# Hybrid NSA, SGU, S5 and expert layers: remaining parts on GpSimd, gates in column groups, four banks for the last rows, output sent by tile

## What is computed

```
for l in range(2):
    h = rms_norm(x, norm_mix_g[l])
    q, k_c, v_c, k_s, v_s, k_w, v_w, nsa_g, sgu_in, s5_in, branch_g = split(h @ w_in[l])
    nsa_gates = sigmoid(nsa_g)                       # 24 columns: 8 heads x 3 branches
    y_a = nsa_attention(q, ..., nsa_gates, positions) @ w_attn_o[l]   # compressed, selected, window
    y_b = spatial_gating(sgu_in, ...) @ w_sgu_o[l]
    y_c = s5_layer(s5_in, ...) @ w_s5_o[l]
    g_a, g_b, g_c = split(sigmoid(branch_g))
    x = x + (g_a * y_a + g_b * y_b + g_c * y_c) @ w_mix_o[l]
    h = rms_norm(x, norm_ffn_g[l])
    x = x + hierarchical_moe(h, ...)                 # 4 groups x 8 experts, top 2 of one group
return rms_norm(x, norm_final_g)
```

## Time and profile before

| | |
|---|---|
| median of 3 runs | 1936.79 us (1935.34 to 1937.72) |
| the profiled execution, its own time | 1934.61 us |
| its span in the trace | 1932.8 us |
| busy share PE / DVE / ACT / POOL | 97% / 51% / 25% / 7% |
| granted TensorE clock, mean | 0.986 of full speed |
| DMA moved | 482.13 MB, 427 GB/s in the slices of the expert phases |

### The profile page before, as it was taken

One profiled execution on the slowest core, in us unless ns is written; L12 is line 12 of the kernel. 1 busy time (PEld: TensorE's weight loads), 2 busy tenths in 40 slices (PEclk: granted clock), 3 DMA queues, 4 the chain that ended last, 5 costly groups with the idle time before them and its releaser, 6 DMA issues. The chain is left out here.

```text
span 1932.8 us, 26668 instructions
## 1 busy us (share of the span) xinstructions
PE 1865.5 (97%) x10360; PEld 1170.3 (61%) x10361; DVE 993.6 (51%) x1929; ACT 479.5 (25%) x854; POOL 144.5 (7%) x237
## 2 busy tenths in 40 slices
PE   6999999999999999999899999999999999999995
PEld 4768777778445455454457777777774445455442
DVE  7764655676344343343467555557673344343344
ACT  4403444423111111111234134444321111111112
POOL 3600000050000000000063000000400000000000
PEclk9999999999999999999989999999999999999998
DMA  4222111253999999999712221114359999999993
GB/s 168 66 81 78 66 66 66 89 159 145 378 427 427 424 427 425 427 428 420 310 50 85 76 83 66 66 45 123 125 218 403 427 427 426 425 425 424 426 428 154
DMA packets 59952, 482.13 MB, mean 249 GB/s; under 512 B 9808, under 2 KB 22608, under 8 KB 30672
## 3 DMA queue, kind: packets, MB, share of 16 engines
q1 hardware_dynamic: 59856, 480.80, 61.3%
HBM read 476.59 MB, written 4.19 MB: 249 GB/s over the span
## 5 line engine op out<-in xcount | busy, mean ns | idle before, releaser
L1877 DVE TENSOR_TENSOR x_tokens<-x_tokens,ps 128x512 f32<-128x512 f32 x240 | 161.7, 687 | 236.7 <-PE ps L1041 235.5
L1107 PE MATMUL ps<-arena,branch 128*64 128x512 f32 x512 | 226.6, 595 | 0.0
L1107 PE MATMUL ps<-slabs,branch 128*64 128x512 f32 x512 | 226.6, 595 | 0.0
L1057 PE MATMUL ps<-arena 128*64 128x512 f32 x512 | 225.1, 592 | 0.5 <-DVE arena L1867 0.5
L1057 PE MATMUL ps<-slabs,arena 128*64 128x512 f32 x512 | 225.0, 592 | 0.5 <-issue 0.5
L1058 PE MATMUL ps<-arena 128*64 128x512 f32 x512 | 225.1, 592 | 0.0
L1058 PE MATMUL ps<-slabs,arena 128*64 128x512 f32 x512 | 225.0, 592 | 0.0
L779 PE MATMUL ps<-h_hi,w_parts 128*128 128x512 f32 x768 | 210.8, 408 | 1.5 <-DVE w_parts L1490 1.5
L1057 PEld LDWEIGHTS ps<-slabs,arena 128*64 128x64 f32 x512 | 70.1, 137 | 146.5 <-issue 146.4
L779 PEld LDWEIGHTS ps<-h_hi,w_parts 128*128 128x128 f32 x768 | 135.1, 189 | 38.8 <-issue 9.2
L1057 PEld LDWEIGHTS ps<-arena 128*64 128x64 f32 x512 | 70.0, 137 | 145.9 <-issue 145.9
(11 more groups left out here) (353 smaller groups left out, 3129.2 us busy)
## 6 DMA issues: line engine op xcount, KB each, us to landing
arena<-in_expert_w_gate SPq DMA_DIRECT2D x32, 2048.0 KB, 12.2
slabs<-in_expert_w_gate SPq DMA_DIRECT2D x32, 2048.0 KB, 15.1
slabs<-in_expert_w_up SPq DMA_DIRECT2D x32, 2048.0 KB, 19.6
arena<-in_expert_w_up SPq DMA_DIRECT2D x32, 2048.0 KB, 16.7
arena<-in_expert_w_down SPq DMA_DIRECT2D x32, 2048.0 KB, 9.5
slabs<-in_expert_w_down SPq DMA_DIRECT2D x32, 2048.0 KB, 14.0
slabs<-in_gate_w SPq DMA_DIRECT2D x24, 1024.0 KB, 4.8
slabs<-in_dense SPq DMA_DIRECT2D x22, 1024.0 KB, 5.8
```

What stands on the lines that cost most here:

```text
L1057: nc.tensor.matmul(ps[0:64, BANK_GU[b], :], xk, low[:, k, :], start=(k == 0), stop=(k == ND - 1), tile_position=(0, 0))
L1107: done = nc.tensor.matmul(ps[64 * b:64 * b + 64, BANK_Y[half], :], hidT[:, k, CAP * b:CAP * (b + 1)], w_down[b][:, k, half * 512:(half + 1 ...
L1877: v.tensor_tensor(xs, xs, ps[:, BANK_BACK[n % 2], :], ALU.add).then_inc(s["back_added"], 1)
```

## The change

Six parts, in both layers unless said:

1. **Prologue.** DVE's angle operations stand between the scalings of tiles (`scale_token(t)`), ACT takes the root of tile t-1 after the square of tile t, and sin is computed before the last angle operations for cos. POOL builds a 128x24 matrix `stack` of four 24-column pieces of the identity, one for each group of 32 rows.
2. **Gates.** `nsa_job` keeps 32 columns of weights as the stationary operand in one of four column groups (`tile_position=(0, r)`), and moves 128 tokens of `hT`; contraction step k goes to group k % 4. ACT copies the 128x512 result to SBUF (`nsa_parts`), and `nsa_sums()`, placed after the two S5 jobs, adds the four groups with four matmuls against `stack`. Tanh stands later on ACT, after `s5_evac(1)`.
3. **Rotation** of index u - 2 in place of u - 1, so each one job later.
4. **Remaining parts.** `low_part` goes from DVE to POOL, in half tiles: a multiplication (L2110: x, read with a stride, by 1/rms) and a subtraction (L2111) of 128x512 each, 16 operations for a layer. `gather_tile` waits for its half tile.
5. **Last quad.** Returned rows use four PSUM banks in place of two; `add_back(0)` stands behind `hid_of(1)`; in the final pair only rows 0 to 3 come before the hidden transposes, then the first half of the down product, rows 4 to 7, and the second half.
6. **Output** (last layer). SP sends each tile in the layer's own block as soon as it is scaled; the last block only waits.

```
 def square_tokens(act, g, arrived):
...
                 nc.scalar.activation(x_unit[:, t, :], x[:, t, :], ACT.Square, accum_out=sumsq[:, t:t + 1]).then_inc(g["sq"], 1)
-                act.wait_ge(g["var"], t + 1)
-                nc.scalar.activation(rstd[:, t:t + 1], sumsq[:, t:t + 1], ACT.Sqrt).then_inc(g["sd"], 1)
+                if t >= 1:
+                    root(t - 1)
+            root(NT - 1)
...
-                reduce_angle(nc, link, ang, kk, rr, r2)
-                scale_tokens(dve, turn_g, False)
+                turns_of(nc, link, ang, kk)
+                link(nc.vector.scalar_tensor_tensor(rr, kk, -PI_1, ang, ALU.mult, ALU.add))
+                scale_token(dve, turn_g, 0, False)
+                link(nc.vector.scalar_tensor_tensor(rr, kk, -PI_2, rr, ALU.mult, ALU.add))
+                scale_token(dve, turn_g, 1, False)
+                link(nc.vector.scalar_tensor_tensor(rr, kk, -PI_3, rr, ALU.mult, ALU.add))
+                link(nc.vector.tensor_scalar(rr, rr, PI_SAFE, -PI_SAFE, ALU.min, ALU.max))
+                scale_token(dve, turn_g, 2, False)
+                scale_token(dve, turn_g, 3, False)
+                quarter_from(nc, link, rr, r2)
...
                     if last_layer:
                         sp.dma_start(gfin, io["gfin"].to_broadcast([P, D])).then_inc(s["gfin_in"], 16)
                         sp.wait_ge(s["gfin_in"], 16)
+                        for t in range(NT):
+                            sp.wait_ge(s["next_xn"], t + 1)
+                            sp.dma_start(io["out"][0, t * P:(t + 1) * P, :], x_unit[:, t, :]).then_inc(fin, 16)
...
                         for k in range(ND):
-                            last = nc.tensor.matmul(ps[:, BANK_S[0], t * 24:(t + 1) * 24], hT[:, k, t * P:(t + 1) * P], wnsa[:, k, :],
-                                                    start=(k == 0), stop=(k == ND - 1))
+                            r = 32 * (k % 4)
+                            last = nc.tensor.matmul(ps[r:r + 32, BANK_S[0], t * P:(t + 1) * P], wnsa[k], hT[:, k, t * P:(t + 1) * P],
+                                                    start=(k < 4), stop=(k >= 4), tile_position=(0, r))
+                        last.then_inc(s["nsa_done"], 1)
+
+                    def nsa_sums():
+
+                        pe.wait_ge(s["nsa_parted"], 1)
+                        for t in range(NT):
+                            last = nc.tensor.matmul(ps[:, BANK_S[1], t * 24:(t + 1) * 24], nsa_parts[:, t * P:(t + 1) * P], stack, start=True, stop=True)
                         last.then_inc(s["nsa_done"], 1)
...
-                        if 1 <= u <= 6:
-                            rotate(u - 1)
+                        if 2 <= u <= 7:
+                            rotate(u - 2)
...
-                                pe.wait_ge(s["x_lo_ready"], t + 1 + (half if t == NT - 1 else 0))
+                                pe.wait_ge(s["x_lo_ready"], 2 * t + half + 1)
...
+                        banks = BANK_BACK_LAST if last_quad else BANK_BACK
+                        final = last_quad and at == 3
+                        for n in range(4 if final else 8):
                             if not first:
                                 if n >= 2 or not second:
-                                    back_free(i, n)
-                                row_back(n)
+                                    back_free(i, n, 4 if final or last_quad and n >= 2 else 2)
+                                row_back(n, banks)
...
+                        down_half(i, 0)
+                        if final:
+                            for n in range(4, 8):
+                                back_free(i, n, 4)
+                                row_back(n, banks)
+                        down_half(i, 1)
...
-                    def low_part(t, lo, hi):
-
-                        dve.wait_ge(s["x_hi_ready"], t + 1)
-                        to, of = (a[:, t, :].rearrange("q (k p) -> q k p", k=ND)[:, lo:hi] for a in (x_lo, x_hi))
-                        xs = x[:, t, :].rearrange("q (p k) -> q k p", k=ND)[:, lo:hi]
-                        v.scalar_tensor_tensor(to, xs, rstd[:, t:t + 1], of, ALU.mult, ALU.subtract).then_inc(s["x_lo_ready"], 1)
...
+                    def low_part(t, half):
+
+                        ks = slice(4 * half, 4 * half + 4)
+                        xs = x[:, t, :].rearrange("q (p k) -> q k p", k=ND)[:, ks]
+                        unit, hi, lo = (a[:, t, :].rearrange("q (k p) -> q k p", k=ND)[:, ks] for a in (xn, x_hi, x_lo))
+                        link(g.tensor_tensor(unit, xs, rstd[:, t:t + 1].unsqueeze(2).to_broadcast([P, 4, P]), ALU.mult))
+                        g.tensor_tensor(lo, unit, hi, ALU.subtract).then_inc(s["x_lo_ready"], 1)
+
+                    for t in range(NT):
+                        pool.wait_ge(s["x_hi_ready"], t + 1)
+                        for half in range(2):
+                            low_part(t, half)
...
-                for t in range(NT):
-                    sp.dma_start(io["out"][0, t * P:(t + 1) * P, :], x_unit[:, t, :]).then_inc(fin, 16)
                 sp.wait_ge(fin, 16 * NT)
```

More of the change, by code:

```diff
@@ L2176, in _ @@
                     def _(dve):
-                        scale_tokens(dve, turn_g, last_layer)
+                        for t in range(NT):
+                            scale_token(dve, turn_g, t, last_layer)
                     @block.tensor
```

112 lines of the change are left out of this document (70 added, 42 removed).

## The result

| | before | after |
|---|---|---|
| median of 4 runs | 1936.35 us (1935.34 to 1937.72) | 1921.73 us (1920.38 to 1923.66) |
| ratio, 95% interval | | 0.9928 [0.9914, 0.9942] |
| profiled execution, its own time | 1934.61 us | 1923.66 us |
| span | 1932.8 us | 1921.9 us |

The change makes the kernel 14.6 us (0.7%) faster. The forecast was 1912.7 us with 1897 to 1920: the direction was right, and the time lies 9 us over the forecast and 1.7 us over the range.

The account below looks back on a forecast made before the run. Edits pay in PE's own work, its waits or the two ends; 1934.61 - 11.2 - 12.2 - 0.7 - 2.4 - 4.8 + 7.2 = 1910.5 us, 1912.7 by the median, range 1897 to 1920.

Parts of the forecast that it names:

- Gates: Gate jobs, both layers: shorter matmuls and the clock staying up behind them, 11.2 us gained, 6.6 if the clock falls.
- Rotation: First rotation, both layers: PE's wait for DVE goes and the clock returns, 12.2 us gained; 7.9 without the clock.
- Prologue: Start of the kernel: scaled tiles come sooner and PE's transposes end earlier, 0.7 us gained (0.3 to 1).
- Last quad: Last expert pair of each layer: PE's waits for a free bank go, twice 1.2 us gained.
- Output: End of the kernel: tiles leave earlier and the last transfer lands in 3.8 us, 4.8 us gained (3.6 to 5.7).
- Remaining parts on POOL: Routing, both layers: POOL's reads delay DVE's routes and PE waits, 3.6 us a layer, 7.2 us lost in all.
- Turn-taking: Forecast case, 54%: in routing, DVE's small two-input operations wait for whole POOL operations; 1912.7 us, own range 1908 to 1919.
- the rival in which it does not come back elsewhere: Rival, 12%: low clock stays at gates and rotation, and falls behind new waits; 1923 us, range 1917 to 1926.
- small operations are not held: Rival, 30%: POOL does not hold DVE's small routing operations, 4.7 us gain for 7.2 loss; 1900.8 us, 1898 to 1903.
- The slower one: Rival, 3%: POOL's strided operations so slow that the gather waits at its last tile; about 1946 us at 4 us each.
- the lower end of its own range, 1908: Forecast case's fastest time, said to come from the unstrided POOL price and the output's bounds.
- the 1.8 us price: Routing: the first POOL operation of each pair, strided, taking 1.8 us, for a loss of 6.4 us a layer.

Follow-up runs that it names:

- gates_one_sum: The kernel before with the gate part alone and one of its four summing matmuls for each layer; 1921.91 us, ratio 0.9932.
- only_pool: The kernel before with the remaining parts moved to POOL and nothing else; 1948.16 us, ratio 1.0076.
- pool_writes: The changed kernel with POOL's two operations for each half tile replaced by five memsets that read nothing; 1906.12 us, ratio 0.9851.
- only_gates: The kernel before with the gate part alone, including the small POOL block that builds `stack`; 1929.69 us, ratio 0.9976.
- after_pair: The changed kernel with the gate jobs of tiles 0 and 1 joined, eight matmuls fewer for each layer; 1917.39 us, ratio 0.9909.
- between_pad16: The kernel with POOL's work placed where DVE does not route, plus 16 already met PE waits before `rank(3)`; 1903.43 us, ratio 0.9838.
- between_pad32: The kernel with POOL's work placed where DVE does not route, plus 32 already met PE waits before `rank(3)`; 1907.36 us, ratio 0.9852.

## Why the prediction was right or wrong

- **Gates: right in mechanism and size, but for what they do to the code.** 2.4 us for the jobs where 2.76 was forecast, and the clock stayed up behind them. `gates_one_sum`, with a short branch and 1.3 us of matmuls too few, is 13.1 us faster than before (10 to 16); less 1.3, 11.8 against 11.2 forecast. That the sizes meet is luck in part: the 4.6 us for the clock were read from one execution in which it fell behind the old gates in both layers, while over the six profiled kernels with the old gates it did so in six places of twelve. With the new gates it did so in none of twenty-two.
- **Rotation: right.** 12.2 us forecast and measured alone, the waits gone and the clock up behind them.
- **Prologue: too small a term, it seems**, 0.7 us (0.3 to 1) against 3 us (1 to 5) alone. Why it is more than the trace's 1.3 us at the in-projection is open; a low clock came in half of the executions there and not in the others.
- **Last quad: not to be told** from nothing alone (forecast 2.4, interval -1.5 to 5.6).
- **Output: too small a term**, 4.8 against 7.2 us (4 to 10) alone, 6.1 in its trace, since a transfer issued by itself landed in 2.6 us and not 3.8. In the changed kernel PE's branch ends the program instead and leaves 3.7.
- **Remaining parts on POOL: the step that failed most.** Turn-taking was the right case: the small operations are held. But the forecast's term, "3.6 us a layer, 7.2 us in all", is 14.7 us alone (10.6 to 19) and 9.3 (medians) to 16 (traces) in the change. It had two waits. PE's wait at `route_logits(1)` was 2.55 for 2.1 us; the held TENSOR_SCALAR, 0.92 us longer than free, was not counted. The wait for `rank(3)` grew by 1.26 us, as forecast within 0.3. These two make 3.8 of the 7.9 us that PE lost in layer 1's routing. The other 4 us, which the term did not have at all, go with the clock: it fell behind the first wait (6.58 us busy at 0.56, 2.9 us lost) and was low for longer before the experts. The forecast had put a low clock after these waits only in the rival in which it does not come back elsewhere. In the four executions in which POOL reads while DVE routes it fell behind both waits in both layers, sixteen places of sixteen. Behind the old wait of about 1.7 us for `rank(3)`, in the eight kernels with the parts on DVE, it fell in eight places of sixteen.
- **The branch: a step that was missing.** The forecast's sum went over engines' work and waits in the program's stages and took the layer's end as it stood. With the gate part PE's branch takes 3.3 to 4.1 us and not 0.35; 3.5 us at the boundary and 2.4 at the end (5.5 against 3.1 us from the last scaling to the end of the span).

Put together from the parts alone: -3.1 (prologue) - 11.8 (gates) - 12.2 - 1.9 (quad) - 7.2 (output) + 14.7 + 5.9 (branches) = -15.6 us, against 13.9 to 14.6 measured; the intervals of the parts hold the difference. Against the forecast's -24.1 that is 7.5 us for the part on POOL and 5.9 for the branches, less 5 us by which the prologue, the gates, the output and the last quad together gave more than forecast. The miss of 9 us would have been larger without these.

Of the rivals, that small operations are not held fell by the trace. That the clock would not come back at gates and rotation fell too; the measured 1921.7 lies in that rival's range of 1917 to 1926, but by coincidence, since of its reasons only the low clock behind the new waits came true. The slower one asked for 3.7 us for each POOL operation; they took 1.28 to 1.47, the strided multiplication 0.1 us more than the subtraction. Two figures of the forecast do not follow from what it names: the lower end of its own range, 1908, of which the output's bound gives 0.9 us, and the 6.4 us a layer for the 1.8 us price.

Shown by experiments: that the part on POOL costs what it does through its reading while DVE routes (`only_pool`, `pool_writes`, `between`); that the gate part makes the branch long, and that fewer matmuls ahead of it make it short (`only_gates`, `gates_one_sum`, `after_pair`). Read from all the traces: that a long branch holds a transfer of instructions and a short one does not. Only argued: that it hangs on where the branch's target lies in PE's code whether that transfer has to be waited for. Instructions added by `between_pad16` and `between_pad32` left it long, which neither shows nor rules that out.

## What to carry to other kernels

Before work moves from DVE to POOL, look at what DVE does at that time, not at how busy it is: a chain of tiny operations on the critical path paid 0.9 to 1.1 us here for each of the four steps that a POOL operation held, and then PE's clock pays again. With three tiles of the same POOL work placed where DVE does not route, and the fourth on DVE (`between`), the kernel was 6.8 us faster than with all of it on DVE. And when a part that looked right in its own stage brings less than it should, lay the two traces beside each other to the very end of a layer: control code that no one edited can have changed its length.

## What the runs showed of the hardware that was not expected

- A DVE TENSOR_SCALAR with one tensor input, on 4 columns, was held by a reading POOL operation (1.15 us for 0.23) and a TENSOR_SCALAR on 32 columns once by a POOL memset (0.67 for 0.24); operations with two SBUF inputs were not held by memsets at all. The forecast had drawn on the Trainium skill (page "SBUF — State Buffer", section "SBUF: two separate sides"), by which the shared ports are locked for a whole instruction, and the trace agrees, down to 4 columns.
- POOL's read of x with a stride of 8 elements cost 1.39 us for 128x512 against 1.29 for the unstrided subtraction; ACT's strided read of such a tile took up to 2.30 us for 1024 elements where its unstrided square took 1.07.
- A branch of PE over code that is not run took 0.35 us in nine kernels and 3.3 to 4.1 us in seven others, short or long in both layers of a kernel alike, and three summing matmuls for each layer decided between the two. The long ones hold a transfer of instructions of some 16 KB that starts about 1 us after the branch.
- PE's clock fell to its lower level behind waits of 2.5 and 2.96 us in sixteen places of sixteen, though PE was busy on both sides of them; over 54 us of the same routing without them (`between`) it stayed at 1.00.
